# A router on rows that are not yet scaled, modulation chunks in pairs, and a more even filling of an attention loop

## The reference

```python
h = rms_norm(x, g_mix);  x = x + hybrid_mixer(h, ...)      # 8 + 4 heads, then two gates, w_pa, w_pb, w_o
h = rms_norm(x, g_moe);  x = x + hier_moe(h, ...)
# hier_moe
gl = h @ w_group + b_group;  gp = softmax(gl);  g_idx = argmax(gl);  g_w = gp[g_idx]     # 4 groups
el = (h @ w_expert)[group g_idx] + b_expert[g_idx];  ep = softmax(el)                    # 8 experts in it
vals, idx = top_k(ep, 2);  weights = g_w * vals / sum(vals)
out[token] += weight * ((silu(xb @ w1[e]) * (xb @ w3[e])) @ w2[e])                       # 32 experts
# second block
mod = silu(c) @ w_ada + b_ada          # 1024 -> 3072: shift, scale and gate of the block
```

## Time and profile before

| | us |
|---|---|
| median of three runs | 1055.93 |
| the profiled execution | 1055.72 |
| its span, first to last instruction | 1053.9 |
| TensorE busy | 989.2 (94%) |
| VectorE, ScalarE, GpSimd busy | 393.3, 368.7, 125.2 |

### The profile page before, as it was taken

One profiled execution on the slowest core, in us unless ns is written; L12 is line 12 of the kernel. 1 busy time (PEld: TensorE's weight loads), 2 busy tenths in 40 slices (PEclk: granted clock), 3 DMA queues, 4 the chain that ended last, 5 costly groups with the idle time before them and its releaser, 6 DMA issues.

```text
span 1053.9 us, 14601 instructions
## 1 busy us (share of the span) xinstructions
PE 989.2 (94%) x6197; PEld 690.7 (66%) x6197; DVE 393.3 (37%) x761; ACT 368.7 (35%) x606; POOL 125.2 (12%) x79
## 2 busy tenths in 40 slices
PE   7999997999999999999999898876999999999996
PEld 6888886965434443443333333336999999999994
DVE  4454446845111111121211111125334444774464
ACT  4546664541111111111111111115445555554443
POOL 1111020120000000000000000001321111351122
PEclk9999998998999999999999999996999999999998
DMA  8973644697999999999999999995555545445300
GB/s 277 382 263 143 239 162 161 225 421 300 412 420 419 420 419 419 419 419 420 419 420 419 420 419 420 418 401 215 179 212 187 187 141 187 161 160 195 145 2 40
DMA packets 84043, 307.92 MB, mean 292 GB/s; under 512 B 6623, under 2 KB 13176, under 8 KB 59392
## 3 DMA queue, kind: packets, MB, share of 16 engines
q1 hardware_dynamic: 80184, 302.16, 73.2%
q10 hardware_dynamic: 3784, 4.73, 1.4%
HBM read 305.81 MB, written 2.63 MB: 293 GB/s over the span
## 4 chain that ended last, share of the span: by engine, by line
PE 65%; SPq 17%; DVE 8%; ACT 4%; DMA 3%; issue 2%; POOL 1%; POOLq 0%; ACTq 0%; DVEq 0%
PE bank L778 63%; SPq L830 17%; DMA ring<-in_w 3%; DVE arena L1253 2%; DVE arena L1256 2%; DVE wR L1253 2%; DVE arena L1259 1%; ACT wR L1835 1%; PE bank L1202 1%; ACT arena L2011 1%; PE bank L965 1%; POOL small L2175 1%; POOL wR L2187 0%; DMA arena<-in_x 0%; PE bank L959 0%
## 5 line engine op out<-in xcount | busy, mean ns | idle before, releaser
L778 PE MATMUL bank<-hTR,wR 128*128 128x256 f32 x2520 | 316.2, 286 | 5.6 <-DVE hTR L1253 2.3
L778 PEld LDWEIGHTS bank<-hTR,wR 128*128 128x128 f32 x2520 | 307.9, 193 | 10.0 <-issue 5.1
L778 PE MATMUL bank<-ring,arena 128*64 128x512 f32 (+1 forms) x1040 | 224.8, 596 | 8.9 <-DMA ring<-in_w 8.0
L1835 ACT ACTIVATE wR<-ring 128x1024 fp32r<-128x1024 f32 x161 | 168.3, 1054 | 109.8 <-PE bank L778 108.0
L1253 DVE TENSOR_TENSOR wR<-ring,wR 128x1024 fp32r<-128x1024 f32 x125 | 155.3, 1247 | 136.1 <-ACT wR L1835 135.7
L778 PE MATMUL bank<-arena 128*64 128x512 f32 (+8 forms) x794 | 169.0, 535 | 6.3 <-DMA arena<-in_w 3.4
L778 PEld LDWEIGHTS bank<-ring,arena 128*64 128x64 f32 (+1 forms) x1040 | 68.7, 135 | 141.3 <-issue 128.8
L1253 DVE TENSOR_TENSOR arena<-arena,bank 128x256 f32<-128x256 f32 (+1 forms) x36 | 16.1, 450 | 349.1 <-ACT arena L2011 347.4
L1990 ACT ACTIVATE arena<-bank 64x512 f32<-64x512 f32 x64 | 37.9, 593 | 288.7 <-PE bank L778 288.4
L2187 POOL TENSOR_TENSOR wR<-ring,wR 128x1024 fp32r<-128x1024 f32 x36 | 87.9, 2440 | 331.3 <-ACT wR L1835 331.3
L778 PEld LDWEIGHTS bank<-arena 128*64 128x64 f32 (+5 forms) x794 | 65.2, 149 | 90.8 <-issue 83.4
(11 more groups left out here) (207 smaller groups left out, 811.6 us busy)
## 6 DMA issues: line engine op xcount, KB each, us to landing
ring<-in_w SPq DMA_DIRECT2D x120, 1024.0 KB, 25.8
arena<-in_w SPq DMA_DIRECT2D x72, 1024.0 KB, 25.5
ring<-in_w_in SPq DMA_DIRECT2D x29, 2048.0 KB, 9.0
ring<-in_w_ada SPq DMA_DIRECT2D x5, 2048.0 KB, 9.2
ring<-in_w_o SPq DMA_DIRECT2D x2, 2048.0 KB, 7.8
ring<-in_w_o_attn SPq DMA_DIRECT2D x2, 2048.0 KB, 7.8
ring<-in_w_o_conv SPq DMA_DIRECT2D x2, 2048.0 KB, 8.2
ring<-in_w_out SPq DMA_DIRECT2D x2, 2048.0 KB, 9.2
```

Source lines behind the costliest of these rows:

```text
L778: return pe.e.matmul(o, l, r, start=start, stop=stop)
L1835: eng.activation(h, w, ACT.Copy).then_inc(s_high, 1)
```

## The change

**Router on unscaled rows.** `turn2` transposes the unscaled rows XN, in halves of 512 columns: the first half inside w_o's second chunk, the second half after it. g_moe is multiplied into the router's weights once, in the attention loop (`s_wg`). `logits` has tokens as rows at once, so the way back (`lgT`) is gone; the token's factor is applied when the logits are read from the bank. The mean square is taken in four halves by ScalarE. The softmaxes leave the chain of the choice: the greatest logits are chosen directly, and `weights()` computes the weights after the first four gathers have been read.

**Gather on unscaled rows.** XShR and XSlR are split from XN, in halves; three of the four low halves are GpSimd's, one is VectorE's. `slot_factors` (16 matmuls of two columns for four experts) brings each slot's weight and factor to its row; silu, the product of H and the eviction of y apply them, in place of the scaling of Y by the weight.

**Ada in pairs.** Two chunks are multiplied into one bank (columns of SC32 that are zero but for one keep them apart) and have one sum with two columns. Chunks 0 to 3 are in the loop now, 4 and 5 behind the logits. The arena place at 8 is no longer a slot.

**Filling.** The loop's first call of the generator is made in rounds 1, 3, 5, 7 and 8 to 15, and no more in 0, 2, 4 and 6. The generator holds 32 pieces.

The diff, cut to its core:

```diff
-        chunks += [gate[0], ada[0], gate[1], ada[1], gate[2], gate[3]]
+        chunks += [gate[0], ada[0], ada[1], gate[1], ada[2], ada[3], gate[2], gate[3]]
...
-        chunks += ada[2:]
-        slots += [RING + 3, free_next[0], free_next[1], free_next[2]]
+        chunks += ada[4:]
...
                 if g in (1, 2):
-                    b = ada(g - 1)
-                    yield
+                    b = PB.use(("adaw", g - 1), PR.next()).bank
+                    for m in (1, 0):
+                        O1.add("ada", g - 1, m)
+                        yield
+                    for m in (1, 0):
+                        O1.loads.release(f"ada{2 * g - 2 + m}")
...
-            if i < 16:
+            if i > 7 or i % 2:
                 next(fill, None)
...
             for st in O1.chunk(f"wo{c}", uses, "y"):
                 O1.add(*st)
+                if c and st[3] == 0:
+                    for n in range(NT):
+                        PB.use(("hT2", 0, n), 2 + n)
+                    O1.add("turn2", 0)
+                elif c and st[3] == 1:
+                    O1.add("xsplit", 0)
+                elif c and st[3] == 2:
+                    PB.use("lg", 7)
+                    O1.add("logits", 0)
             O1.add("evict", f"wo{c}", None)
+        for n in range(NT):
+            PB.use(("hT2", 1, n), 4 + n)
+        O1.add("turn2", 1)
+        O1.add("logits", 1)
...
+            elif what == "turn2":
+                c = a[0]
+                for n in range(NT):
+                    u = U_["hT2", c, n]
+                    may_write(pe, u)
+                    emptied(pe, U_[f"wo{c}", n])
...
+            elif what == "logits":
+                c, u = a[0], U_["lg"]
+                may_write(pe, u)
+                pe.wait_ge(s_wg, 1)
+                for n in range(NT):
+                    emptied(pe, U_["hT2", c, n])
+                    for j in range(4 * c, 4 * c + 4):
+                        last = mm(pe, banks[u.bank][:, 256 + 40 * n:292 + 40 * n], hT[:, j, 128 * n:128 * n + 128], wr[:, j, :],
+                                  j == 0 and n == 0, j == 7 and n == 1)
...
+            def slot_factors(b, bank):
+
+                pe.wait_ge(s_weights, 1)
+                for i in range(EB):
+                    for n in range(NT):
+                        for h in range(2):
+                            last = mm(pe, bank[64 * h:64 * h + 64, 256 + 2 * i:258 + 2 * i],
+                                      PmR[:, b % 2, n, 64 * i:64 * i + 64].bitcast(F32), WR[:, n, EB * b + i, :], n == 0, n == 1)
+                return last
...
+                    v.wait_ge(s_rs[n], 2)
+                    x, f = BL[:, 256 + 40 * n:292 + 40 * n], ss[:, 4 + n:5 + n]
+                    v.step(stt(g8[:, n, 0:4], x[:, 0:4], f, bias36[:, 0:4], ALU.mult, ALU.add))
+                    last = stt(lg[:, n, 4:36], x[:, 4:36], f, bias36[:, 4:36], ALU.mult, ALU.add)
...
+                v.wait_ge(s_xhigh, 4)
+                tt(by_eights(XSlR[:, 1, :], 1), in_order(XN[:, 1, :], 1), by_eights(XShR[:, 1, :], 1).bitcast(F32),
+                   ALU.subtract).then_inc(s_xlow_dve, 1)
...
-                    tt(H, H, banks[u.bank][:, 256:512], ALU.mult).then_inc(u.free, 1)
+                    emptied(v, factors_of(P, r, e))
+                    stt(H, banks[u.bank][:, 256:512], RW[:, b % 2, k, 1:2], H, ALU.mult, ALU.mult).then_inc(u.free, 1)
...
+            def x_low(c, n):
+                p.wait_ge(s_xhigh, 2 * c + n + 1)
+                eng.tensor_tensor(by_eights(XSlR[:, n, :], c), in_order(XN[:, n, :], c), by_eights(XShR[:, n, :], c).bitcast(F32),
+                                  ALU.subtract).then_inc(s_xlow, 1)
```

More of the change, by code:

```diff
@@ L1062, in ada_pe @@
+        def ada_pe(pe, p, m):
+            u, w = U_["adaw", p], view(f"ada{2 * p + m}")
             may_write(pe, u)
             pe.wait_ge(s_siluc, 2)
-            pe.wait_ge(*landed[f"ada{i}"])
+            pe.wait_ge(*landed[f"ada{2 * p + m}"])
             for k in range(8):
                 g = 32 * (k % 4)
-                last = mm(pe, banks[u.bank][g:g + 32, :], SC32[:, k, :], w[:, k, :], k < 4, k > 3)
-            last.then_inc(u.full, 1)
-        def ada_sum_pe(pe, i):
-            u = U_["ada", i]
+                last = mm(pe, banks[u.bank][g:g + 31 + m, :], SC32[:, k, 1 - m:32], w[:, k, :], m == 1 and k < 4, m == 0 and k > 3)
+            if m == 0:
+                last.then_inc(u.full, 1)
@@ L1122, in gather @@
                                   n == 0 and x is XShR, n == 1 and x is XSlR)
+                if b == 0 and j == 7:
+                    last = slot_factors(0, banks[u.bank])
                 last.then_inc(u.full, 1)
+            def slot_factors(b, bank):
[6 more added lines that the diff above has]
+                return last
             def down(e):
@@ L1466, in route @@
+                last.then_inc(U_["lg"].free, 1)
                 v.settle()
@@ L1576, in experts @@
                     gathered(0, j)
+                if not r:
+                    weights()
                 for e in range(NE):
@@ L1945, in first_steps @@
                         eng.dma_start(XN[:, n, :], x_d[128 * n:128 * n + 128, :]).then_inc(s_x2[n], 16)
-            def ada_rows(i):
-                u = U_["adaw", i]
+                elif what == "turn2":
+                    c = a[0]
+                    square(c, 0)
+                    u = U_["hT2", c, 0]
+                    filled(s, u)
+                    eng.activation(hT[:, 4 * c:4 * c + 4, 0:128], banks[u.bank][:, :].rearrange("p (j t) -> p j t", j=4),
+                                   ACT.Copy).then_inc(u.free, 1)
+                    square(c, 1)
+                elif what == "xsplit":
+                    for n in range(NT):
+                        x_high(0, n)
@@ L1971, in route @@
[L1971 to L1979 removed]
+                s.wait_ge(s_shift, 1)
+                eng.activation(ex5, ex5, ACT.Exp).then_inc(s_rexp, 1)
@@ L2191, in first_steps @@
                     split_low(a[0])
+                elif what == "turn2":
+                    p.settle()
+                    for n in range(NT):
+                        p.wait_ge(s_sq[n], 2 + a[0])
+                        if a[0] == 0:
+                            p.step(eng.tensor_scalar(ss[:, 2 + n:3 + n], ss[:, n:n + 1], 1.0, EPS, ALU.mult, ALU.add))
+                        else:
+                            p.step(eng.tensor_tensor(ss[:, 2 + n:3 + n], ss[:, 2 + n:3 + n], ss2[:, n:n + 1], ALU.add))
+                            p.settle()
+                            rsqrt(ss[:, 4 + n:5 + n], ss[:, 2 + n:3 + n], s_rs[n])
+                elif what == "xsplit":
+                    for n in range(NT):
+                        x_low(0, n)
                 elif what == "diff_out":
```

330 lines of the change are left out of this document (132 added, 198 removed).

## The result

The changed kernel takes 1046.55 us (median of six runs, 1045.01 to 1049.93), the kernel before 1055.31 beside it (six runs, 1053.69 to 1056.77). The ratio is 0.992, with an interval from 0.991 to 0.994: 8.3 us faster by the ratio (8.8 by the medians), where 12.1 were forecast. The profiled execution took 1047.49 us with a span of 1045.7, against 1055.72 and 1053.9.

A forecast was written before the change was run, and what follows sets the result against it. The prediction took the experts' weight stream, its start and its holes, as the bound, with TensorE bounding the time ahead of y. Terms -5.0 (loop) and -7.1 (holes) gave -12.1 us from 1055.72: 1043.6 us, range 1040.5 to 1051.

The forecast's parts named there:

- the loop: Attention loop up to y: waits and slow clock gone, two ada chunks added, early rounds slightly slower; -5.0 us.
- the holes: Gaps in the expert weight stream from 235 to 270 us, 8.1 us together; an earlier first release gains 7.1 us.
- what lies behind the experts: Unchanged work after the experts' stage: moves as a whole, every row earlier by the same 12 us.
- The bound: Experts' stage: ends when its 96 chunks have landed, set by the stream's start and how long it stands still.
- The early rounds: Loop rounds 0, 2, 4 and 6, each losing one of two filling pieces: cost between 0 and 8.4 us, taken as 0.5.
- The router: From w_o's end to the first gather: 11.0 us in place of 21.0, with the gather at 233.5 instead of 245.44.
- rival C: Router's choice late by the port: GpSimd's quarter takes twice its 1.2 us; 1045.4 us, chance 0.13.
- the case of two SBUF inputs beside GpSimd: Router's choice: by the skill's shared-port rule, VectorE's two-input operations would lose the full 1.2 us of GpSimd's quarter.
- A: The forecast itself: earlier stream start and both holes gained, 1043.6 us; chance 0.55.
- B: Stream start does not follow TensorE, y stays at 207.46 behind VectorE's queue, only holes gained: 1048.6 us; chance 0.16.
- E: Load queue blocks: g2's or g3's weights wait behind releases of ada chunks 0 and 1; 1052.6 us, chance 0.08.
- D: Rounds 0 to 7 starve, 16.8 us of waits: 1059.9 us, slower once they wait 12.6 us together; chance 0.08.

The follow-up runs named there:

- the second measurement: The changed kernel measured again, unaltered, against the kernel before: 1050.86 us, ratio 0.995.
- the exchange of the filling rule: Old filling in the changed kernel: 1055.13 us, ratio 0.9995; new filling alone in the kernel before: 1050.13 us, ratio 0.994.
- the half ada: The changed kernel with half of the rows of ada chunks 0 to 3 left out: 1045.67 us, ratio 0.992 to the kernel before.
- the first chunk's experiment: The changed kernel with the first expert chunk in a ring slot free before y: 1049.06 us, ratio 0.995 to the kernel before.
- the kernel with early diagonals: The changed kernel with the diagonals of experts 28 to 31 written before VectorE's wait for silu: 1042.36 us, ratio 0.989 to the kernel before.

## Why the prediction was right in kind, and too large by 3 to 8 us

Seen from the profiled executions: forecast -12.1, measured -8.2. Up to expert 28 it is -7.15, and the rest lies behind it. By the second measurement the time gained is 4 to 5 us, and 7 to 8 were too much. That the medians lie within the range, 1040.5 to 1051, is in part luck: the loop missed by 5.8 us, and the holes gave back 0.9 and what lies behind the experts 1.1.

*The bound.* Right. The experts' stage is set by the stream, its start and its holes; every experiment that moved start or release moved expert 28 by what it should, within 0.5 us, but for the 113 rows in the kernel before (0.5 us where the release moved by 1.6).

*The loop: -5.0 forecast at y, +0.8 measured.* This is the step that failed, and not by its main term. The 6.3 us of waits and the slow clock did go, worth 5 us in both kernels by the exchange of the filling rule; I had counted 9.3, but the changed loop has a wait of 2.04 us of its own for the last head. The two ada chunks cost 3.8 as said. What I did not have: (1) the head. The change adds eight rows of g_moe to the table, 105 to 113, and I read past it. The table lands 2.35 us later (7.06 to 9.41), TensorE has the slow clock behind it, and the forget gate's transposes come 3.1 us late (58.43 to 61.52). (2) The early rounds: taken at 0.5, the one wait of 0.73 us at 75.92 and the slow product behind it (7.51 for 48 matmuls; at 76.17 before it was 6.02) make 2.2; in other traces of the same kernel the 1.5 us of slow clock stand behind the last head's wait. (3) The wait of 2.04 us behind the last softmax, which filling could not reach. Together 3.1 + 2.2 + 3.8 + 2.0 - 9.3 = +1.8, against +0.8 seen; the 1.0 left I can't place. By experiment (1) is worth 2.4 us and (3) 1.5 us.

*The router: right within half a microsecond.* From w_o's end (224.94 + 3.02 = 227.96) to the first gather 10.5 us, forecast 11.0. GpSimd's quarter and the operations of VectorE that it overlaps are, in the changed kernel:

```profile
230.75 1.55 POOL L2223 TENSOR_TENSOR XSlR<-arena,XShR 128x512 fp32r<-128x512 f32 x1
```

```profile
231.30 0.67 DVE L1275 SCALAR_TENSOR_TENSOR arena<-bank,small,brow 128x4 f32<-128x4 f32 x4 [1.17 <-PE bank L778]
231.88 0.23 DVE L1476 MAX8 arena<-arena 128x8 f32<-128x8 f32 x2
```

GpSimd's quarter took 1.55 us where 1.2 was counted. Four operations in 0.67 us and two in 0.23: none stands still, nothing of rival C. But these four read one operand from a bank, the two have only one, and the choice's first operation with both operands in SBUF starts at 232.76, after GpSimd's end at 232.30. So the case of two SBUF inputs beside GpSimd, which the prediction weighed, did not arise, and nothing here speaks for or against it. From the gather to the release 7.3 us in place of 8.6: the product that ends it took 3.78 in place of 4.88 us, since the clock was back sooner (0.89 from 240 to 250 us, where the kernel before has 0.74, and 0.50 in the second half). That is 1.3 us better than forecast, and only margin.

*The holes: -7.1 forecast, -8.0 measured*, with the caution that the start of the margin was misjudged. I took the stream to run dry 41.7 us behind its start, when the eighth chunk has landed. The measured bound is 38.6. Two things make the 3.1 us between them. One is that data take time to come: the kernel before shows it, issue at 254.07, in stretches of one microsecond:

```profile
254.00:255.00 1.00, 1.00 (x10) 0.97 (x8) 0.26 (x1) 0.00 (x0) 0.00 (x0) 1.00 0.00 0
255.00:256.00 1.00, 0.90 (x8) 0.72 (x7) 0.70 (x2) 0.00 (x0) 0.00 (x0) 1.00 0.80 180
256.00:257.00 1.00, 1.00 (x9) 0.58 (x9) 0.95 (x2) 0.00 (x0) 0.00 (x0) 1.00 0.89 319
257.00:258.00 1.00, 1.00 (x8) 0.33 (x6) 0.01 (x1) 0.00 (x0) 0.00 (x0) 1.00 1.06 451
```

No data come for 0.9 us, and with 240 and 101 of 420 GB/s missing in the next two microseconds 1.7 us' worth is lost until the rate is full. The other is that the first release is not the tightest. By the same count the stream of the changed kernel would be dry at 208.29 + 41.7 = 250.0, and with one and two chunks more at 255.0 and 260.0; the releases at 245.72, 252.69 and 258.27 are 4.3, 2.3 and 1.7 us ahead. The third has the least margin, as the expectation of the first chunk's experiment had it (1.2 was measured), and I had looked at the first alone. That these two make up the 3.1 us is an estimate; no run moved the third release without the first. Forecast and measured margin are 2.1 and 1.2 us; had the release been as late as I said (39.6 behind the start) there would have been none, and 1 us of hole.

*Behind the experts: "every row earlier by the same 12 us".* Wrong by the last four experts. I looked at the idle share of 500 to 600 us for cover, and the last experts have more work for TensorE (Y's way back, diagonals, a wait for each). The waits for the diagonals are 0.15 us longer than before each. Behind them the clock falls in some executions; it does so in the trace of the kernel before with the new filling too (5.33 us for 16 matmuls at 668.28), whose waits are not longer, so the 0.15 us are not the reason. In numbers: -7.15 at expert 28 is -5.7 at 679.81, and then -8.2 at the end, as the kernel before has its own slow stretch behind the experts.

*The rivals.* The first median is 3.0 us over A and 2.1 under B (1048.6), and B's sign was that y stays at 207.46. It did, but not by B's mechanism: y did follow TensorE, as the half ada shows (2.7 of the 4.8 us for 3.7 us less work), and TensorE was itself late. E did not occur. D's condition, early rounds that wait, was met by 0.73 us of the 12.6 it needed; a wait for VectorE in rounds 0 to 7 was also among the signs that the forecast would be wrong, and for the loop's term it was right.

## What to carry to other kernels

A stream of loads has several gates (its start, each place that comes free, its first releases). Measure each as a distance from the stream's start, against the distance at which it begins to cost; opening one alone can be worth nothing. When a change adds rows to a small table or data at the head, look at the shape of that transfer as well as at its bytes. And a stage that has just been sped up needs a second look at its last iterations: a wait of 2 us on TensorE's path costs 2 us, and 1.5 to 2.4 us more in executions in which the clock falls behind it.

## What the runs showed of the hardware

- A table of 113 rows of 512 bytes reached its first use at 9.4 and 9.9 us in two kernels, one of 105 at 7.1, and one of 120 was there before 6.6. The Trainium skill, "DMA: Bandwidth & Descriptors", section "Why a DMA increments its semaphore by 16 and not by 1", says that such a transfer uses the largest number of engines up to 16 that divides its slowest dimension. For 105 and 120 that is 15, for 113 (a prime) it is 1. The traces agree in the order of the three; they don't show the engines of that one transfer by themselves.
- The granted clock can fall behind waits far shorter than I expected. In the changed kernel TensorE waited 0.73 us at 75.92, and the stretch around it reads

```profile
70.00:80.00 10.00, 9.27 (x61) 7.82 (x61) 4.73 (x14) 4.88 (x8) 2.39 (x1) 0.92 0.50 182
```

With a wait of 1.9 us in each of the last experts it is below 1.00 too:

```profile
660.00:680.00 20.00, 16.06 (x72) 5.67 (x69) 3.55 (x12) 3.46 (x6) 0.00 (x0) 0.91 1.01 420
```

and 1.00 in the kernel with early diagonals:

```profile
660.00:680.00 20.00, 17.96 (x90) 7.40 (x88) 4.82 (x12) 3.46 (x6) 0.00 (x0) 1.00 1.01 419
```

The columns are as above. The same wait of 0.73 us stands in eleven of the profiled executions; the 48 matmuls behind it took 7.5 us in six of them and 6.0 in five. In four of these five a product with w_pa is slow instead, behind the wait of 2.0 us at the last head. So a short wait goes with the slow clock in some executions and not in others, of one program too. The changed kernel's times lie between 1045 and 1055 us.
- A late engine is later than its delay: 2.9 us of VectorE's work cost 4.7 us at the first gather, and 11.5 cost 13.2, the other 1.8 being TensorE's products at 1.2 GHz.
